# TensorE's order in the expert stage: four gate-and-up quarters, both halves of the preceding down, then the turn

## The reference

```python
out = jnp.zeros_like(t)
for grp in range(N_GROUPS):
    sl = slice(grp * EXPERTS_PER_GROUP, (grp + 1) * EXPERTS_PER_GROUP)
    hid = (jax.nn.silu(jnp.einsum('nd,edf->nef', t, w_e_gate[sl]))
           * jnp.einsum('nd,edf->nef', t, w_e_up[sl]))
    out = out + jnp.einsum('nef,efd->nd', hid * combine[:, sl, None], w_e_down[sl])
```

## Time and profile before

| | before |
|---|---|
| median of 3 runs | 1139.13 us |
| the profiled execution's own time | 1139.23 us |
| its span, first to last instruction | 1137.5 us |
| TensorE busy with matmuls | 1106.9 us, 97% |
| VectorE, ScalarE busy | 508.0 us, 45%; 403.1 us, 35% |
| mean granted TensorE clock | 0.988 |
| expert stage, first L1733 to first L1811 of the last scatter | 597.46 to 1121.62 us |

### The profile page before, as it was taken

The page is one execution under the profiler, slowest core; times in us unless marked ns, Lnnn a source line. Parts: engine busy times, 40 slices in busy tenths (PEclk is TensorE's granted clock), DMA queues, the critical chain, the costliest instruction groups (busy, mean ns, idle before and its releaser), DMA issues.

```text
span 1137.5 us, 13564 instructions
## 1 busy us (share of the span) xinstructions
PE 1106.9 (97%) x4884; PEld 719.6 (63%) x4884; DVE 508.0 (45%) x720; ACT 403.1 (35%) x546; POOL 2.7 (0%) x13
## 2 busy tenths in 40 slices
PE   7999999999999999999979999999999999999995
PEld 6888888788888888888864344634455443644343
DVE  5546555575464554746663222432225222332225
ACT  5335555653433334444331222222232222312224
POOL 0000000000000000000000000000000000000000
PEclk8999999999999999999989999999999999999998
DMA  9554445468666566577538999999999999989962
GB/s 321 197 194 158 157 157 175 163 234 271 204 211 203 184 210 197 171 255 250 191 114 280 407 412 413 350 331 414 414 412 304 350 413 415 369 297 402 413 253 112
DMA packets 105883, 312.12 MB, mean 274 GB/s; under 512 B 13128, under 2 KB 14192, under 8 KB 97136
## 3 DMA queue, kind: packets, MB, share of 16 engines
q1 hardware_dynamic: 105840, 311.54, 74.8%
HBM read 309.41 MB, written 2.10 MB: 274 GB/s over the span
## 4 chain that ended last, share of the span: by engine, by line
PE 92%; DVE 3%; ACT 3%; issue 1%; DMA 0%; DVEq 0%; SPq 0%; ACTq 0%
PE bank L1733 20%; PE bank L1470 18%; PE bank L1471 17%; PE bank L1472 17%; PE bank L1753 10%; PE bank L1782 3%; PE bank L1742 1%; PE bank L1572 1%; PE bank L1674 1%; PE bank L1596 1%; PE bank L1477 1%; PE bank L1793 1%; ACT whi L592 1%; DVE wlo L902 1%; PE bank L1811 1%
## 5 line engine op out<-in xcount | busy, mean ns | idle before, releaser
L902 DVE TENSOR_TENSOR wlo<-raw,whi 128x2048 fp32r<-128x2048 f32 x92 | 210.7, 2291 | 201.1 <-ACT whi L592 201.1
L592 ACT ACTIVATE whi<-raw 128x2048 fp32r<-128x2048 f32 x92 | 176.2, 1916 | 254.6 <-PE bank L1472 254.6
L1733 PE MATMUL bank<-slot,xe 128*64 128x512 f32 x1024 | 247.5, 605 | 0.0
L1470 PE MATMUL bank<-whi,actT_hi 128*128 128x512 f32 x608 | 240.9, 396 | 2.2 <-DVE wlo L902 1.3
L1472 PE MATMUL bank<-wlo,actT_hi 128*128 128x512 f32 x608 | 237.7, 391 | 0.0
L1471 PE MATMUL bank<-whi,actT_lo 128*128 128x512 f32 x608 | 237.7, 391 | 0.0
L1733 PEld LDWEIGHTS bank<-slot,xe 128*64 128x64 f32 x1024 | 62.3, 136 | 133.3 <-issue 129.7
L1470 PEld LDWEIGHTS bank<-whi,actT_hi 128*128 128x128 f32 x608 | 114.7, 189 | 28.6 <-DVE wlo L902 2.9
L1472 PEld LDWEIGHTS bank<-wlo,actT_hi 128*128 128x128 f32 x608 | 114.6, 188 | 24.3
L1471 PEld LDWEIGHTS bank<-whi,actT_lo 128*128 128x128 f32 x608 | 114.7, 189 | 22.8
L1753 PE MATMUL bank<-slot,hT 128*128 128x512 f32 x256 | 125.7, 614 | 0.4 <-ACT hT L819 0.4
(11 more groups left out here) (228 smaller groups left out, 1003.1 us busy)
## 6 DMA issues: line engine op xcount, KB each, us to landing
slot<-in_w_e_gate SPq DMA_DIRECT2D x128, 512.0 KB, 8.7
slot<-in_w_e_up SPq DMA_DIRECT2D x128, 512.0 KB, 10.2
slot<-in_w_e_down SPq DMA_DIRECT2D x64, 1024.0 KB, 10.6
raw<-in_w_gate SPq DMA_DIRECT2D x64, 512.0 KB, 4.4
raw<-in_w_in SPq DMA_DIRECT2D x56, 512.0 KB, 4.7
raw<-in_w_out SPq DMA_DIRECT2D x32, 512.0 KB, 4.8
raw<-in_w_branch_a SPq DMA_DIRECT2D x16, 512.0 KB, 4.7
raw<-in_w_branch_b SPq DMA_DIRECT2D x16, 512.0 KB, 4.4
```

What stands on the lines that cost most here:

```text
L592: return act.activation(whi[slot][:], src, ACT.Copy)
L902: dve.tensor_tensor(wlo[s][:], raw[:, k, :], whi[s][:], ALU.subtract).then_inc(lo_made, 1)
L1470: pe.matmul(o, x_hi, w_hi, start=start, stop=False)
L1733: mm = pe.matmul(dst[h * CAP:(h + 1) * CAP, :], xe[:, kt, r, :], w[:, :, k, :], start=kt < 2, stop=kt >= KT - 2)
```

## The change

TensorE does the four quarters of expert j, then `down_0` and `down_1` of expert j - 1 whole, then `turn_hidden(j)`. Experts 0 and 1 have no such predecessor: their quarters come first, the scatter between them, then turn, down_0 and down_1 of expert 0, and the turn of expert 1. The gather of the next group follows the last turn in one piece, before the last expert's down; `gather_weights` of the next group ends the group (in group 0 it stands behind the quarters of expert 0). The places of the pieces in the ring, the order of loads and the order of work on ACT and DVE follow. No matmul, copy or load is added or taken away. Long runs of removed lines are cut.

```diff
--- before.py
+++ after.py
@@ -333,11 +333,11 @@
 
         def gate_up_at(j, k4):
 
-            return k4 if j == 0 else 6 * j - 2 + (0, 1, 3, 4)[k4]
+            return k4 if j == 0 else 6 * j - 2 + k4
 
         def down_at(j, f):
 
-            return 6 * EPG - 2 + f if j == EPG - 1 else 6 * j + 4 + (2, 5)[f]
+            return 6 * EPG - 2 + f if j == EPG - 1 else 6 * j + 8 + f
 
         PIECES = 6 * EPG
         DOWNS = [down_at(j, f) for j in range(EPG) for f in range(2)]
@@ -463,11 +463,11 @@
             after_raw(1)
             load_gate_up(1, 1, 0)
             after_raw(2)
+            load_gate_up(1, 2, 0)
+            after_raw(3)
+            load_gate_up(1, 3, 0)
+            await_used(sp, DENSE - 2)
             load_down(0, 0, 0)
-            after_raw(3)
-            load_gate_up(1, 2, 0)
-            await_used(sp, DENSE - 2)
-            load_gate_up(1, 3, 0)
             await_used(sp, DENSE - 1)
             load_down(0, 1, 0)
             load_gate_up(2, 0, 0)
@@ -482,24 +482,19 @@
 
             def load_first(i, e):
 
+                after_gate_up(i - 1, EPG - 2, 2)
+                load_gate_up(0, 0, e)
+                after_gate_up(i - 1, EPG - 2, 3)
+                load_gate_up(0, 1, e)
                 after_down(i - 1, EPG - 3, 0)
-                load_gate_up(0, 0, e)
-                after_gate_up(i - 1, EPG - 2, 2)
-                load_gate_up(0, 1, e)
-                after_gate_up(i - 1, EPG - 2, 3)
                 load_gate_up(0, 2, e)
                 after_down(i - 1, EPG - 3, 1)
                 load_gate_up(0, 3, e)
-                after_gate_up(i - 1, EPG - 1, 0)
-                load_gate_up(1, 0, e)
-                after_gate_up(i - 1, EPG - 1, 1)
-                load_gate_up(1, 1, e)
+                for k4 in range(4):
+                    after_gate_up(i - 1, EPG - 1, k4)
+                    load_gate_up(1, k4, e)
                 after_down(i - 1, EPG - 2, 0)
                 load_down(0, 0, e)
-                after_gate_up(i - 1, EPG - 1, 2)
-                load_gate_up(1, 2, e)
-                after_gate_up(i - 1, EPG - 1, 3)
-                load_gate_up(1, 3, e)
                 after_down(i - 1, EPG - 2, 1)
                 load_down(0, 1, e)
                 after_down(i - 1, EPG - 1, 0)
@@ -509,24 +504,19 @@
 
             def load_rest(i, e):
                 after_gate_up(i, 0, 0)
+                load_gate_up(2, 2, e)
+                after_gate_up(i, 0, 1)
+                load_gate_up(2, 3, e)
+                after_gate_up(i, 0, 2)
                 load_down(1, 0, e)
-                after_gate_up(i, 0, 1)
-                load_gate_up(2, 2, e)
-                after_gate_up(i, 0, 2)
-                load_gate_up(2, 3, e)
                 after_gate_up(i, 0, 3)
                 load_down(1, 1, e)
                 for j in range(3, EPG):
-                    after_gate_up(i, j - 2, 0)
-                    load_gate_up(j, 0, e)
-                    after_gate_up(i, j - 2, 1)
-                    load_gate_up(j, 1, e)
+                    for k4 in range(4):
+                        after_gate_up(i, j - 2, k4)
+                        load_gate_up(j, k4, e)
                     after_down(i, j - 3, 0)
                     load_down(j - 1, 0, e)
-                    after_gate_up(i, j - 2, 2)
-                    load_gate_up(j, 2, e)
-                    after_gate_up(i, j - 2, 3)
-                    load_gate_up(j, 3, e)
                     after_down(i, j - 3, 1)
                     load_down(j - 1, 1, e)
                 for f in range(2):
@@ -835,22 +825,21 @@
                 for j in range(EPG - 1):
                     gate_low(i, j)
                     silu(i, j)
+                    hidden_turned(i, j)
+                    down_hi(i, j)
                     if j == 1:
                         act.wait_ge(selT_full, i + 1)
                         act.activation(selT[:], bank[6][:, 0:T], ACT.Copy).then_inc(selT_made, 1)
-                    hidden_turned(i, j)
-                    down_hi(i, j)
                 last = EPG - 1
                 gate_low(i, last)
+                silu(i, last)
+                hidden_turned(i, last)
                 if another_follows:
                     gathered_a(i + 1, 0)
-                silu(i, last)
-                if another_follows:
                     gathered_a(i + 1, 2)
-                hidden_turned(i, last)
+                    gathered_a(i + 1, 4)
                 down_hi(i, last)
                 if another_follows:
-                    gathered_a(i + 1, 4)
                     gathered_a(i + 1, 6)
                 else:
                     output_hi(i)
@@ -1390,31 +1379,35 @@
                     output_lo(i - 1)
                 weights(i)
                 if after_another:
-                    add(i - 1, range(8), SCATTER)
+                    add(i - 1, range(0, 1), SCATTER)
                 else:
                     find_left()
-                for j in range(EPG - 1):
+                gate_sum(i, 0)
+                if after_another:
+                    add(i - 1, range(1, 3), SCATTER)
+                hidden(i, 0)
+                if after_another:
+                    add(i - 1, range(3, 8), SCATTER)
+                hidden_lo(i, 0)
+                down_lo(i, 0)
+                for j in range(1, EPG - 1):
                     gate_sum(i, j)
                     hidden(i, j)
+                    hidden_lo(i, j)
+                    down_lo(i, j)
                     if j == 1 and another_follows:
                         dve.wait_ge(selT_full, i + 1)
                         pick(i + 1)
                         pick_pairs(i + 1)
-                    hidden_lo(i, j)
-                    down_lo(i, j)
                 last = EPG - 1
                 gate_sum(i, last)
+                hidden(i, last)
+                hidden_lo(i, last)
                 if another_follows:
-                    gathered_v(i + 1, 1)
-                hidden(i, last)
-                if another_follows:
-                    gathered_v(i + 1, 3)
-                hidden_lo(i, last)
+                    for q in range(1, KT // 2, 2):
+                        gathered_v(i + 1, q)
                 down_lo(i, last)
-                if another_follows:
-                    gathered_v(i + 1, 5)
-                    gathered_v(i + 1, 7)
-                else:
+                if not another_follows:
                     output_lo(i)
                     add(i, range(8), SCATTER_LAST)
 
@@ -1743,31 +1736,27 @@
                                    start=True, stop=True)
                 mm.then_inc(hT_full, 1)
 
-            def down_0(i, j, blocks):
+            def down_0(i, j):
 
                 n = down_at(j, 0)
-                if blocks[0] == 0:
-                    pe.wait_ge(hT_made, 2 * EPG * i + 2 * j + 1)
-                    pe.wait_ge(slot_in[n % RING], arrived(i, n))
-                for b in blocks:
+                pe.wait_ge(hT_made, 2 * EPG * i + 2 * j + 1)
+                pe.wait_ge(slot_in[n % RING], arrived(i, n))
+                for b in range(NC):
                     mm = pe.matmul(bank[2 + b][:], hT_0[:], slot[n % RING][:, b * COLS:(b + 1) * COLS],
                                    start=(j == 0), stop=False)
-                if blocks[-1] == NC - 1:
-                    mm.then_inc(d0_used, 1)
...
-                    pe.wait_ge(d_lo_made, EPG * i + j + 1)
+                mm.then_inc(d0_used, 1)
+
+            def down_1(i, j):
+
+                pe.wait_ge(hT_lo_made, EPG * i + j + 1)
+                pe.wait_ge(d_lo_made, EPG * i + j + 1)
                 last = j == EPG - 1
-                for b in blocks:
+                for b in range(NC):
                     cols = slice(b * COLS, (b + 1) * COLS)
                     mm = three(bank[2 + b][:], hT_hi[:], hT_lo[:], d_hi[:, cols], d_lo[:, cols], False, last)
                     if last and b < 3:
                         mm.then_inc(o_full, 1)
-                if blocks[-1] == NC - 1:
-                    mm.then_inc(d1_used, 1)
+                mm.then_inc(d1_used, 1)
 
             def gather(i, qs):
 
@@ -1812,62 +1801,47 @@
                     pe.matmul(bank[dst][:], selT[:, tok], o_lo[:, cols], start=False, stop=True).then_inc(scat_full, 1)
 
             def group_t(i, after_another, another_follows):
-                gate_up(i, 0, 0)
-                gather_weights(i)
-                gate_up(i, 0, 1)
+                for k4 in range(4):
+                    gate_up(i, 0, k4)
                 if after_another:
                     pe.wait_ge(selT_made, i)
                     scatter(i - 1, range(0, 4), SCATTER)
+                    pe.wait_ge(cw_made, 3 * i + 3)
+                    scatter(i - 1, range(4, 6), SCATTER)
                 else:
+                    gather_weights(i)
                     count_left()
-                gate_up(i, 0, 2)
-                if after_another:
```

(94 more changed lines are left out.)

## The result

The changed kernel takes 1110.77 us (median of 4 runs, 1109.95 to 1111.53), against 1139.25 us before (4 runs): a ratio of 0.9749, 95% interval 0.9732 to 0.9766. The profiled execution took 1111.53 us, its span is 1109.7 us, 27.8 less than before. All of it lies in the expert stage, which lasts 496.3 us in place of 524.2; ahead of it and behind it the two kernels agree within 0.1 us.

The account below looks back on a forecast made before the run. TensorE was taken as bound by its own matmul stream. Savings of 3.6 us in group 0, 14.0 in groups 1 and 2 and 9.5 in group 3, together 27.1, took 1139.23 to 1112 us, range 1106 to 1118.

Parts of the forecast that it names:

- The run of quarters: Four gate and up quarters in a row on TensorE, up to the next kind: 7.015 us, against 7.48 before.
- Rival C: Borders between matmul kinds cost nothing by themselves, so the 24 steady experts gain nothing: 1140 us, chance 0.03.
- The steady expert: Experts 2 to 7 of each group, 24 in all: 13.89 us each instead of 14.93, together 25.0 us less.
- The border of down_0 with down_1: Passing from down_0 to down_1 in a steady expert: taken as nothing, at worst 0.1 us.
- No new waits for hid or d_lo in experts 2 to 7: Turn and down_1 find operands ready: 6.3 us before the turn for hid, 11 us for d_lo, which needs 5.2.
- Uncovered down of the first expert: Expert 0 of each group, turn to down_1: 5.35 us, including waits of 0.37 for hT_0 and 0.68 for d_lo.
- Gather 8.2 us, weights 1.89: At a group's end: the gather in one piece 8.2 us, waits for its copies included; the next group's weights 1.89.
- Group 0: First quarter to the next group's first quarter: 125.85 us against 129.44, 3.6 less, the smallest gain.
- Count behind the weights: In group 0 the count stands right behind the weights and waits for their copies: 0.75 us with the signal.
- A: The loads become the bound in groups after the first; 6 to 12 us come back, 1118 to 1124 us, chance 0.11.
- B: No slot freed for 15 us around the gather, so DMAs idle; slower, 1152 us, chance 0.05.
- The late landing of a down piece: Late in group 3, a down piece's time from issue to landing: 18 us, against 12.1 before.

Follow-up runs that it names:

- the changed kernel again: The changed kernel without any edit, run and profiled a second time as the measure for other kernels: 1109.96 us, ratio 0.9747 to the kernel before.
- the rows of matmuls by themselves: The changed kernel plus, after the last scatter, wait-free matmul rows alternating or repeating kinds; adds some 100 us, only start-to-start times in the rows count.
- F with R: In those added rows, one float32 product of 128 x 128 alternating with two fp32r products of 128 x 128: period 1.33 us.
- the earlier turn: Against the changed kernel, each group's scatter units 6 and 7 and turn of expert 0 moved between quarters 1 and 2 of expert 1: 1104.76 us.

## Why the prediction was right

- **Forecast.** 1112 was foretold, 1110.8 measured, by the mechanism named. That the number is so close is in part luck: in the profile of the changed kernel again, without the low clock, the stage takes 1092.15 - 597.55 = 494.6 us where the terms add up to 497.3, and in the profile of the result 1.7 us of low clock, which no term had, made up for most of this.
- **The run of quarters, 7.015 us.** Measured 7.02. The row of three quarters in group 0 carried this term alone, and the rows of matmuls by themselves repeat it, 5.37 us for three. Rival C falls with it.
- **The steady expert, 13.89 us.** Measured 13.86; 24 times 1.07 is 25.7 against the 25.0 of the sum. The border of down_0 with down_1, taken as nothing, is 0.02 a round trip in the rows by themselves (F with R).
- **No new waits for hid or d_lo in experts 2 to 7.** None is listed. The waits of TensorE in the changed stage are those five pairs and the count's.
- **Uncovered down of the first expert, 5.35 us from turn to down_1.** Measured 621.90 - 616.44 = 5.46 in group 0, the border of 0.1 before the turn included, which the sum had apart. The turn of expert 1 did not wait. What these two waits cost was nevertheless put too low for whoever wants to take them away, as the earlier turn showed.
- **Gather 8.2 us, weights 1.89.** Measured 716.43 - 708.42 = 8.01 and 724.40 - 722.62 = 1.78, probably because both rows before stood at a border with quarters that the new neighbours spare; the weights' 16 matmuls are 1.96 us long behind a quarter and 1.85 behind down_1, in the changed kernel too. With the 0.04 us by which each of six experts is shorter this makes 0.5 of the 0.8 us by which groups 1 and 2 came out shorter; the rest is spread over terms rounded up.
- **Group 0, 125.85 us.** In the profile of the result it was 126.86: the stretch at a granted clock of 0.53 stands in it with 8.78 - 7.09 = 1.7 us, and without it 125.2 is left; the profile of the changed kernel again, at a clock of 1.00 there, has 722.69 - 597.55 = 125.14. That is short of the sum as groups 1 and 2 are. The clock had no term in my sum, and no rival named it.
- **Count behind the weights.** A wait of 0.75 was foretold, 0.71 is listed.
- **The loads.** Rivals A and B did not come. The late landing of a down piece was put at 18 us; from 1037 to 1085 us of the changed kernel it is 14.2:

```profile
slot<-in_w_e_down SPq DMA_DIRECT2D x6, 1024.0 KB, 14.2
```

The margin against A was real but thinner than the text had it: 3.6% more load was still free, 7.3% went past it, and it gives out where ACT reads half 1 of a down, a read for which the prediction worked out no cushion of its own.

## What to carry to other kernels

Where narrow (64-column) and full-width matmuls share TensorE, count the changes of width and not the matmuls: each round trip cost 0.35 us here, while one between float32 and fp32r at full width cost 0.02. Group them as far as the buffers allow, and look for a stretch of the old trace that happens to have the order you want: it prices the new one. When the bound engine gets faster, follow each kind of loaded piece to its first reader, which may be another engine that wants it earlier.

## What the runs showed of the hardware

- The round trip between column widths costs the same 0.35 us whether one or both column halves were busy, so it is not a loss of their running side by side.
- After the same 10 us of work the granted clock fell to 0.53 for 3.4 us in one execution of the changed kernel and stayed at 1.00 in another; it fell in four of the eight profiled executions with that order of work. In the first it cost 1.7 us, 0.15% of the time.
- A wait of TensorE costs more than its listed idle time: 1.03 us for a listed 0.68, and an estimated 0.53 for a listed 0.37.
